# Block products of sums in two matmul stages, and a reordered stage before the recurrence, in a two-block fp32 kernel

## Chip, cores and metric

One core of a Trainium2 chip. The metric is the device time of one execution in microseconds (us), median of the runs. All data are fp32.

## The reference, cut to what matters

The program computes a first block (attention and a mixture of experts, two layers) and then a second block on the 512 tokens it leaves, with D = 1024. The change touches the end of the first block and two stages of the second:

```
h = rmsnorm(x, pre_mix_g)                              # x: result of the first block (layer norm of ALPHA * h_mid + gate * experts)
y_gla, y_sc, y_dil = recurrence(h), convolution(h), dilated_attention(h)
br = stack([y_gla, y_sc, y_dil])                       # each 512 wide
proj = einsum('bsgc,gcd->bsgd', br, w_branch)
gates = sigmoid(h @ w_gate + b_gate)                   # (512 x 1024) @ (1024 x 3072)
merged = sum(gates * proj, axis=2)
x = x + rmsnorm(merged @ w_mix_out, post_mix_g)
h = rmsnorm(x, pre_ffn_g)
gt = causal_dwconv(h @ w_ff_gate) + b
y = (gelu(gt) * (h @ w_ff_up)) @ w_ff_down             # (512 x 2816) @ (2816 x 1024)
x = x + rmsnorm(y, post_ffn_g)
```

## The kernel before

The program is a row of phases. Each phase is one block in which the queues SP, POOL, PE (TensorE), ACT (ScalarE) and DVE (VectorE) run their own hand-written lists of instructions, tied by semaphores; a phase begins when every queue has ended the one before. P = 128 partitions, C = 8 slices of the 1024 channels, NLAT = 4 tiles of 128 tokens, LAT = 512 tokens. `Steps` makes an engine wait for its own last instruction. Weights of the second block go through `ring`, two slots of 2 MB: job j lies in slot j % 2 (`load_weights`, L1983), and a load is issued by SP once the last product of job j - 2 is done.

**combine_turn_phase (L1772 to L1953)** ends the first block. For each token tile t it loads two rows of expert results and `h_mid` (L1804), weighs and adds them (ACT L1848, DVE L1892), multiplies by the gate, adds `h_mid` (L1895, L1896), takes the mean and variance (L1897 to L1899), normalises (ACT L1852, L1854; DVE L1903, L1904, L1911, L1912), takes the root of the mean square (ACT L1858, L1860), and turns the tile with PE by a product with a diagonal matrix `diag` that holds the inverse root (DVE L1919, L1920; PE L1950), after which ACT moves the eight turned pieces to `hT` (L1867). Between the turns PE computes the values of tiles 0 and 1 for the recurrence with ring slot 1 (`values`, L1942). SP issues the rows of tiles 0 and 1, the load of job 1, the first two rows of tile 2, ... in the order of L1802 to L1813, so job 1 stands ahead of tile 2 and job 0 ahead of tile 3 on its queue; then come 16 small loads for the recurrence (L1815 to L1828), on whose arrival it waits before it stores `h` (L1831).

**recurrent_phase and rope_phase** follow and are unchanged. The rope phase already computes its products in the form that the change brings to the gates, with seven block products in place of eight; for that it has made four sums of token halves, in the memory of `merged`.

**merge_phase (L2555 to L2769)** has 48 steps n in three branches i of 16. In the first 8 steps of a branch PE makes a gate chunk of 128 outputs (L2618: 8 matmuls of 128x512), which ACT takes with a sigmoid (L2689); in the next 8 a branch product (L2628: 4 matmuls), which DVE multiplies with the gates and adds to `merged` (L2737, L2740). Products go in turn to two PSUM banks `pa`. Into the even and odd steps up to n = 33 the dilated attention is woven, one unit u = n // 2 of head and query tile at a time: scores (PE L2636), mask and maximum (DVE L2749, L2752), exp (ACT L2694), scaling (DVE L2759), transposes (PE L2648), moves (ACT L2704), weighing of the values (PE L2661), taking (ACT L2709). POOL has nothing to do in this phase.

**feed_forward_phase (L2776 to L3097)**: mixing product (L2884), norms and transposes (L2894), then for each of NF = 22 chunks f of 128 hidden outputs the products of gate and up in seven block products (L2908: 28 matmuls of 256 columns), the first of them copied by ACT (L2990), all joined by DVE (`post`, L3055 to L3058), convolution (ACT L2992, DVE L3081, L3083), gelu (L2994), product (L3090). PSUM is four pieces `banks` of 1024 columns; chunk f uses pieces 0 and 1 where f is even, 2 and 3 where it is odd. The sums of weights are made by POOL for the first pair (L2835) and by DVE after that (L3067). The down product (L2941 to L2956) runs over PASSES = tiles (0, 1), then 2, then 3, each over the 22 chunks, with 1 MB of down weights per two chunks in four slots made of the ring (L2848); a tile's norm, residual and store follow (L2964 to L2965, L3094 to L3097, L2870).

Of the kernel before, what the change touches and what calls it, by code (L numbers as in the profile page):

```python
# [18 lines left out]
ALU = mybir.AluOpType  # L19
# [4 lines left out]
P = 128  # L24
# [1747 lines left out]
def combine_turn_phase(nc, g, l, share, gain, hT, rc):  # L1772
# [4 lines left out]
    with Phase(nc) as ph:  # L1777
# [6 lines left out]
        diag = ph.sb("diag", [P, 2, P])  # L1784
# [3 lines left out]
        row_in = ph.sems("row_in", NLAT)  # L1788
# [3 lines left out]
        weighted, var_ready, root_ready, norm_ready, n_ready, h_made, h_stored, rooted, scaled, turned, moved = (  # L1792
            ph.sem(n) for n in ("weighted", "var_ready", "root_ready", "norm_ready", "n_ready", "h_made", "h_stored", "rooted", "scaled", "turned", "moved"))
# [6 lines left out]
        def _(sp):  # L1800
            ph.clear_other_pool(sp)
            for t in range(NLAT):  # L1802
                for j, src in enumerate((g["y"][tile(t), :], g["y"][tile(t + NLAT), :], g["h_mid"][tile(t), :])):
                    sp.dma_start(y[:, t, j], src).then_inc(row_in[t], 16)  # L1804
                if t == 0:
                    sp.dma_start(gate[:], g["mods"][l, 0:1, 5 * D:6 * D].broadcast_to([P, D])).then_inc(gate_in, 16)
                if t == 2:
                    load_weights(sp, g, 0)
                if t == 1:
# [3 lines left out]
                    load_weights(sp, g, 1)  # L1813
# [26 lines left out]
        def _(act):  # L1840
# [4 lines left out]
            def weigh(t):  # L1845
                if t < NLAT:
                    act.wait_ge(row_in[t], 48)
                    act.activation(y[:, t, 0], y[:, t, 0], ACT.Copy, scale=share[:, t, 0:1]).then_inc(weighted, 1)  # L1848

            def norm(t):  # L1850
                act.wait_ge(var_ready, t + 1)
                act.activation(mv[:, t % 2, 2:3], mv[:, t % 2, 1:2], ACT.Sqrt, bias=eps[:, 0:1]).then_inc(root_ready, 1)  # L1852
# [3 lines left out]
            def root(t):  # L1856
# [3 lines left out]
                act.activation(ss[:, t % 2, 1:2], ss[:, t % 2, 0:1], ACT.Sqrt, scale=1.0 / D, bias=eps[:, 1:2]).then_inc(rooted, 1)  # L1860

# [19 lines left out]
            move(NLAT - 1)  # L1881

        @block.vector
        def _(dve):
# [9 lines left out]
            def residual(t):  # L1894
                step(dve.tensor_tensor(y[:, t, 0], y[:, t, 0], gate[:], ALU.mult))  # L1895
                step(dve.scalar_tensor_tensor(out=y[:, t, 0], in0=y[:, t, 2], scalar=ALPHA, in1=y[:, t, 0], op0=ALU.mult, op1=ALU.add))  # L1896
# [17 lines left out]
            def scale(t):  # L1914

                dve.wait_ge(rooted, t + 1)
                if t >= 2:
                    dve.wait_ge(turned, t - 1)
                step(dve.reciprocal(ss[:, t % 2, 1:2], ss[:, t % 2, 1:2]))  # L1919
                dve.tensor_scalar(diag[:, t % 2], g["ident"][:], ss[:, t % 2, 1:2], None, ALU.mult).then_inc(scaled, 1)  # L1920
# [12 lines left out]
            scale(NLAT - 1)  # L1933

        @block.tensor
        def _(pe):
            def values(t):
# [3 lines left out]
                for i in range(C):  # L1941
                    last = pe.matmul(pV[t][:], hT[:, i, tile(t)], ring[:, 1, i, :], start=(i == 0), stop=(i == C - 1))  # L1942
                last.then_inc(valued, 1)

            for t in range(NLAT):
# [609 lines left out]
def merge_phase(nc, g, hT, yT, QK, dv, merged, mask, bias):  # L2555
# [3 lines left out]
    NU = H * NLAT  # L2559

# [20 lines left out]
    with Phase(nc) as ph:  # L2581
# [11 lines left out]
        turned, moved, weighed, o_out, order = (ph.sem(n) for n in ("turned", "moved", "weighed", "o_out", "order"))  # L2593
        block = ph.block()
        ring, ring_in, ident = g["ring"], g["ring_in"], g["ident"]

        def last_output(j):
# [628 lines left out]
```

## Time and profile before

| | |
|---|---|
| median of 3 runs | 3357.71 us (3355.45 to 3358.58) |
| the profiled execution | 3354.14 us |
| its span in the trace | 3352.3 us |
| mean granted clock of TensorE | 0.945 of full speed |
| busy: PE, DVE, ACT, POOL | 85%, 37%, 23%, 16% of the span |

In the page, PE is a TensorE matmul and PEld the load of its stationary operand, which overlaps the matmul. An fp32 matmul leaves two records in the trace, a transpose one. Matmuls are pipelined, so the duration of one record (592 ns for 512 columns) is longer than the time from one to the next; the time of a stretch of matmuls divided by their count is the price of a record. Times of day are us from the start of the span.

### The profile page before, as it was taken

The page shows a single profiled execution, that of the slowest core. Times are in us where ns is not written, and L with a number is a line of the kernel's source. Part 1 is how long each engine was busy: PE and PEld are TensorE (multiplying, and loading weights), DVE is VectorE, ACT ScalarE, POOL GpSimd, SP SyncE. Part 2 cuts the span into 40 slices and gives each one's busy share as a digit, 9 for nine tenths or more (in the row PEclk, how much of TensorE's full clock was granted, in tenths as well). Part 3 has the DMA queues.
Part 4 walks back from the last instruction along what each step waited for, and adds up shares of the span by engine and source line. Part 5 has one row for each costly group of instructions (what it writes and reads, how often), then busy time and mean ns, then how long its engine had stood idle before and what let it go on. Part 6 is the DMA issues. An engine that isn't in the chain of part 4 may idle for free. (4 is left out here: it accounts for less than half of the span.)

```text
span 3352.3 us, 53098 instructions
## 1 busy us (share of the span) xinstructions
PE 2833.0 (85%) x21873; PEld 1738.4 (52%) x21873; DVE 1239.9 (37%) x2476; ACT 770.7 (23%) x1501; POOL 538.7 (16%) x664
## 2 busy tenths in 40 slices
PE   7998889588776698885867663899999999999999
PEld 4555655344343345653433332445886554588844
DVE  3424856311111343755111112634761331355501
ACT  2224651112111322630111111420212331211100
POOL 0003630233322001521323221010000000100000
PEclk9999999699998899997989887999999999999999
DMA  8833012999999652025999997221222112322337
GB/s 310 310 143 118 1 76 88 380 397 426 426 426 422 237 126 97 3 94 216 382 425 424 424 423 315 72 77 59 101 76 75 51 51 75 114 76 82 119 126 263
DMA packets 188535, 679.24 MB, mean 203 GB/s; under 512 B 52766, under 2 KB 94222, under 8 KB 163782
## 3 DMA queue, kind: packets, MB, share of 16 engines
q1 hardware_dynamic: 176446, 655.56, 50.2%
q0 software_dynamic: 11808, 21.03, 1.7%
q8 instruction: 134, 2.20, 0.3%
q14 instruction: 43, 0.35, 0.0%
q10 hardware_dynamic: 104, 0.10, 0.0%
HBM read 653.89 MB, written 33.98 MB: 205 GB/s over the span
## 5 line engine op out<-in xcount | busy, mean ns | idle before, releaser
L1756 DVE TENSOR_TENSOR hh<-hs,pH 128x128 f32<-128x128 f32 x118 | 33.9, 287 | 774.6 <-ACT hs L1739 774.6
L1719 PE MATMUL pH<-w,room 128*32 128x256 f32 x4224 | 253.9, 395 | 54.5 <-DMA w<-in_moe_w 54.2
L1719 PE MATMUL pH<-room 128*32 128x256 f32 x3328 | 213.5, 414 | 90.1 <-DMA room<-in_moe_w 67.0
L942 POOL TENSOR_SCALAR E<-E,st 128x768 f32<-128x768 f32 (+3 forms) x80 | 168.0, 2100 | 644.7 <-DVE st L1192 644.1
L1719 PEld LDWEIGHTS pH<-w,room 128*32 128x32 f32 x4224 | 140.8, 114 | 158.3 <-issue 77.2
L1719 PEld LDWEIGHTS pH<-room 128*32 128x32 f32 x3328 | 115.0, 120 | 181.0 <-issue 97.2
L419 PE MATMUL pa<-aT,w 128*128 128x512 f32 x416 | 205.8, 599 | 1.3 <-DVE aT L693 1.3
L1727 PE MATMUL pY<-w,hT 128*32 128x256 f32 x2112 | 129.2, 385 | 76.8 <-DVE hT L1759 61.0
L2618 PE MATMUL pa<-hT,ring 128*128 128x512 f32 x384 | 169.7, 598 | 0.0
L987 PE MATMUL pT<-ident,E 128*128 128x128 f32 x672 | 112.7, 287 | 54.9 <-ACT PT L1097 31.3
L2952 PE MATMUL banks<-ring,aT 128*128 128x512 f32 x352 | 151.2, 592 | 0.0
L1727 PE MATMUL pY<-room,hT 128*32 128x256 f32 x1664 | 100.6, 382 | 54.3 <-DVE hT L1759 54.3
L2094 PE MATMUL pa<-hT,ring 128*128 128x512 f32 x320 | 143.8, 606 | 0.0
L1017 PE MATMUL pS<-wout,oT 128*128 128x512 f32 x320 | 141.4, 594 | 0.8 <-issue 0.8
L1727 PEld LDWEIGHTS pY<-w,hT 128*32 128x32 f32 x2112 | 62.7, 110 | 142.8 <-DVE hT L1759 101.6
L1739 ACT ACTIVATE hs<-pH 128x128 f32<-128x128 f32 x118 | 32.7, 277 | 450.6 <-PE pH L1719 450.6
L1675 POOL DMA_INDIRECT y<-y,at_y x122 | 125.8, 1031 | 60.2 <-POOL at_y L1695 59.1
L1742 ACT ACTIVATE y<-pY 128x256 f32<-128x256 f32 x118 | 45.2, 383 | 346.2 <-PE pY L1727 340.7
L987 PEld LDWEIGHTS pT<-ident,E 128*128 128x128 f32 x672 | 71.3, 142 | 99.9 <-issue 47.5
L956 PE MATMUL pS<-room 64*128 64x256 f32 (+2 forms) x608 | 109.3, 476 | 8.3 <-ACT E L1086 4.9
L2618 PEld LDWEIGHTS pa<-hT,ring 128*128 128x128 f32 x384 | 72.4, 192 | 84.4 <-issue 84.4
L2952 PEld LDWEIGHTS banks<-ring,aT 128*128 128x128 f32 x352 | 66.9, 190 | 83.8 <-issue 83.7
(557 smaller groups left out, 4760.4 us busy)
## 6 DMA issues: line engine op xcount, KB each, us to landing
w<-in_moe_w SPq DMA_DIRECT2D x144, 2048.0 KB
room<-in_moe_w SPq DMA_DIRECT2D x48, 2048.0 KB
mw<-in_mod_w SPq DMA_DIRECT2D x24, 2048.0 KB, 16.6
ring<-in_w_ff_down SPq DMA_DIRECT2D x33, 1024.0 KB, 4.9
ring<-in_w_in SPq DMA_DIRECT2D x15, 2048.0 KB, 8.4
ring<-in_w_gate SPq DMA_DIRECT2D x6, 2048.0 KB, 8.4
wf<-in_w_ff_gate SPq DMA_DIRECT2D x11, 1024.0 KB, 5.7
wf<-in_w_ff_up SPq DMA_DIRECT2D x11, 1024.0 KB, 8.0
```

The source lines that it names most:

```text
L419: last = pe.matmul(pa[n % 2][:, 0:512], w[:, i % SLOTS_W, k, tile(c)], aT[:, k, 0:512], start=(k == 0), stop=(k == C - 1))
L942: pool.tensor_scalar(e, e, st[:, u % 4, 6 + b:7 + b], None, ALU.mult).then_inc(readyP, 1)
L956: return pe.matmul(pS[u % 2][:, at:at + w], qT[rows, p, tile(n)], kT[rows, k_chunk(p), k0:k0 + w], start=True, stop=True)
L987: last = pe.transpose(pT[:, tile(j)], E[:, u % NB, b, tile(i)], ident[:])
L1017: last = pe.matmul(pS[n % 2][:, half * 512:(half + 1) * 512], oT[:, k, tile(n)], wout[:, k, half * 512:(half + 1) * 512], start=(k == 4), ...
L1675: pool.indirect_dma_start(out=y_rows, out_offset=bass.IndirectOffsetOnAxis(ap=at_y[:, b:b + 1], axis=0), in_=y[:, b], in_offset=None, boun ...
L1719: last = pe.matmul(pH[strip(s), 0:2 * P].rearrange("p (j n) -> p j n", j=2), xT[:, k, :], slot_of(g, "w13", b)[:, :, k, s * P:(s + 1) * P] ...
L1727: last = pe.matmul(pY[strip(s), 0:YW], hT[:, k, :], slot_of(g, "w2", b)[:, k, s * YW:(s + 1) * YW], start=(k == 0), stop=(k == HC - 1))
L1742: act.activation(y[:, b], pY[:, 0:YW], ACT.Copy).then_inc(y_moved, 1)
L2094: last = pe.matmul(pa[b][:], ring[:, j % RING, i, tile(c)], hT[:, i, :], start=(i == 0), stop=(i == C - 1))
L2618: last = pe.matmul(pa[b][:], ring[:, j % RING, k, (c % 4) * P:(c % 4 + 1) * P], hT[:, k, :], start=(k == 0), stop=(k == C - 1))
L2952: last = pe.matmul(banks[b][:, h * 512:(h + 1) * 512], aT[:, f, tile(t)], wd[:, m % SLOTS_D, f % 2, h * 512:(h + 1) * 512], start=(f == 0) ...
```

## The change

Three parts, in one diff.

**Gates.** Two neighbouring gate chunks c, c + 1 of a branch, the two halves of the channels and the two halves of the tokens form a product of two by two blocks. It is computed with seven products of blocks (each 4 matmuls of 128x256) of sums, in place of eight blocks (16 matmuls of 128x512). DVE makes four sums of weights per pair ahead of it (`sums`, four operations of 512 elements; the last overwrites the weights in the ring); the four sums of tokens are those of the rope phase for branch 0 and are made by POOL (four operations of 1024 elements, in memory of Q and K that heads 0 and 1 no longer need) for branches 1 and 2. The seven products go to the two banks `pa` in four turns (two, two, two and one product). ACT copies the first of them (`copy_first`), DVE adds (`add_first`, three operations of 256 elements; `add_then`, two of 256 and one of 512), and ACT takes both sigmoids of a pair one after the other at the next even step.

**Down product.** Tiles 0 and 2 are computed together in one pass of 11 pairs of chunks, seven matmuls of 512 columns per pair in place of eight; tiles 1 and 3 follow in passes of their own, as tiles 2 and 3 did. DVE makes four sums of down weights per pair (`down_sums`, 512 elements each) and four sums of tokens in two goes (`down_tokens`, of 768 and 640 elements). The order of the rows out is 0, 2, 1, 3.

**The stage before the recurrence.** The rows of all four tiles stand ahead of both weight loads on SP's queue; `h_mid` has a semaphore of its own, so the weighing doesn't wait for it; the table of Sqrt is asked for at the start; the turn is a transpose of rows that ACT has scaled (`scale`) in place of a product with a diagonal; `gather` and the roots are moved earlier in the lists; the values of tile 1 are split round the turn of tile 3, and both copies of values come last.

```diff
@@ combine_turn_phase
             for t in range(NLAT):
                 for j, src in enumerate((g["y"][tile(t), :], g["y"][tile(t + NLAT), :], g["h_mid"][tile(t), :])):
-                    sp.dma_start(y[:, t, j], src).then_inc(row_in[t], 16)
+                    sp.dma_start(y[:, t, j], src).then_inc(mid_in[t] if j == 2 else row_in[t], 16)
...
-                if t == 2:
-                    load_weights(sp, g, 0)
...
-                    load_weights(sp, g, 1)
+            load_weights(sp, g, 1)
+            load_weights(sp, g, 0)
...
+            def scale(t):
+                act.wait_ge(inverse, t + 1)
+                act.activation(y[:, t, 1], y[:, t, 0], ACT.Copy, scale=ss[:, t % 2, 1:2]).then_inc(scaled, 1)
...
+            act.activation(warm[:], eps[:, 0:1], ACT.Sqrt)
             weigh(0)
             weigh(1)
+            deviation(0)
             for t in range(NLAT):
                 norm(t)
+                weigh(t + 2)
                 if t:
                     move(t - 1)
-                weigh(t + 2)
                 root(t)
-                if t >= 2:
-                    take_values(t - 2)
+                deviation(t + 1)
+                scale(t)
             move(NLAT - 1)
+            take_values(0)
+            take_values(1)
...
             residual(0)
+            gather(1)
             for t in range(NLAT):
-                gather(t + 1)
                 factors(t)
-                if t:
-                    scale(t - 1)
                 if t + 1 < NLAT:
                     residual(t + 1)
                 complete(t)
-            scale(NLAT - 1)
+                gather(t + 2)
+                invert(t)
...
                 for k in range(C):
-                    last = pe.matmul(pT[t % 2][:, tile(k)], y[:, t, 0, k::C], diag[:, t % 2], start=True, stop=True)
+                    last = pe.transpose(pT[t % 2][:, tile(k)], y[:, t, 1, k::C], g["ident"][:])
                 last.then_inc(turned, 1)
-                if 1 <= t <= 2:
-                    values(t - 1)
+                if t == 1:
+                    values(0, range(C))
+                if t == 2:
+                    values(1, range(C // 2))
+            values(1, range(C // 2, C))
@@ merge_phase, tensor
+                (a0, a1), (b0, b1) = weights(n)
+                t = token_sums(i)
+                pairs = (((a0, hT[:, lo, first]), (S[1], t[1])), ((S[0], t[0]), (S[2], hT[:, hi, then]))) if n % 2 == 0 else (
+                    ((a1, hT[:, hi, first]), (b0, t[2])), ((b1, t[3]),))
+                for pair in pairs:
+                    if q >= 2:
+                        pe.wait_ge(taken[q % 2], q // 2)
+                    for at, (w, x_cols) in enumerate(pair):
+                        if n % 2 == 0 and at:
+                            pe.wait_ge(s_made, GATES.index(n) // 2 + 1)
+                            if i:
+                                pe.wait_ge(t_made, 1)
+                        for k in range(C // 2):
+                            last = pe.matmul(bank(q)[:, at * HT:(at + 1) * HT], w[:, k, :], x_cols[:, k, :], start=(k == 0), stop=(k == C // 2 - 1))
+                    last.then_inc(product[q % 2], 1)
+                    q += 1
@@ merge_phase, vector
+                    if n < 48 and n % 16 < 8:
+                        add_first(n)
+                else:
+                    if n < 47 and (n + 1) % 16 < 8:
+                        sums(n + 1)
+                    if u < NU:
+                        scale(u)
+                    if n % 16 < 8:
+                        add_then(n)
@@ feed_forward_phase, tensor
+            for m in range(NP):
+                pe.wait_ge(wd_in[m % SLOTS_D], 16 * (m // SLOTS_D + 1))
+                pe.wait_ge(down_t, 1 if m < early_sums else 2)
+                pe.wait_ge(down_s, m + 1)
+                w, s = wd[:, m % SLOTS_D], wf_flat[:, m % 2]
...
+                    if m == 0 and name == "P5":
+                        pe.wait_ge(posted[1], NP)
+                    last = pe.matmul(down_at(name), x_rows, of_w, start=(m == 0), stop=(m == NP - 1))
+                last.then_inc(wd_used, 1)
@@ feed_forward_phase, vector
             for f in range(NF):
                 b, i = f % 2, f // 2 + 1
+                if f == NF - 1:
+                    dve.wait_ge(raised[1], NP - 1)
+                    down_tokens(0, 0, early_sums)
+                    down_sums(0)
                 post(f)
+                if f == NF - 1:
+                    down_sums(1)
...
+            for m in range(2, NP):
+                down_sums(m)
+                if m == early_sums - 2:
+                    down_tokens(1, early_sums, NP)
+            dve.wait_ge(first_taken, 1)
```

## Rows read from the trace of the kernel before

**Rows 1.** The chain of waits that ended last: start, us, what.

```profile
2887.66 0.88 PE banks L2894 x8
...
2949.26 244.78 PE banks L2908 x1120
3194.04 151.08 PE banks L2952 x352
```

**Rows 2.** Busy time by stretch: us, then PE, PEld, DVE, ACT, POOL busy, clock, DMA.

```profile
2066.30:2134.80 68.50, 30.29 (x96) 21.74 (x97) 32.96 (x50) 26.95 (x59) 0.55 (x3) 0.69 0.58 214
...
2546.90:2858.20 311.30, 309.29 (x996) 162.54 (x996) 80.05 (x152) 76.23 (x122) 0.00 (x0) 0.99 0.17 58
2858.20:2921.90 63.70, 62.98 (x168) 30.53 (x168) 17.14 (x32) 14.34 (x34) 10.66 (x4) 0.97 0.51 147
2921.90:3193.90 272.00, 267.21 (x1289) 236.29 (x1290) 151.74 (x200) 42.12 (x71) 0.00 (x0) 0.99 0.26 86
```

**Rows 3.** Groups by line and shape in the merge phase.

```profile
L2618 PE MATMUL pa<-hT,ring 128*128 128x512 f32 x384 | 169.7, 598 | 0.0
...
L2689 ACT ACTIVATE z<-pa,gate_bias 128x512 f32<-128x512 f32 x24 | 16.5, 688 | 53.6 <-PE pa L2618 53.6
L2694 ACT ACT_TABLE_LOAD x9 | 11.5, 1283 | 0.4 <-PEq L91 0.3
```

**Rows 4.** Timeline of a unit with ten keys in the merge phase.

```profile
2646.59 2.31 PE L2636 MATMUL pS<-QK 128*128 128x256 f32 x6
2649.37 1.08 ACT L2704 ACTIVATE PT<-pT 128x512 f32<-128x512 f32 x2 [5.74 <-PE pT L2648]
2649.61 3.60 PE L2628 MATMUL pa<-yT,ring 128*128 128x512 f32 x8
2651.37 1.36 ACT L2694 ACTIVATE E<-E,st 128x1280 f32<-128x1280 f32 x1 [0.91 <-DVE st L2753]
2653.04 1.95 PE L2661 MATMUL pO<-PT,dv 128*128 128x128 f32 x16
```

**Rows 5.** Timeline of the last chunks of the feed-forward phase and the first down products.

```profile
3160.80 1.22 DVE L3067 TENSOR_TENSOR S<-S,wf 128x1024 f32<-128x1024 f32 x1
...
3188.17 0.69 DVE L3090 TENSOR_TENSOR aT<-xg,r 128x512 f32<-128x512 f32 x1 [0.70 <-ACT xg L2994]
...
3193.87 21.62 PE L2952 MATMUL banks<-ring,aT 128*128 128x512 f32 x50
3194.07 0.38 ACT L2990 ACTIVATE r<-banks 128x256 f32<-128x256 f32 x1 [5.93 <-PE banks L2908]
3194.56 0.69 DVE L3055 TENSOR_TENSOR r<-r,banks 128x512 f32<-128x512 f32 x1 [5.70 <-ACT r L2990]
3195.28 0.42 DVE L3056 TENSOR_TENSOR r<-r,banks 128x256 f32<-128x256 f32 x1
...
3196.46 0.69 DVE L3058 TENSOR_TENSOR r<-r,banks 128x512 f32<-128x512 f32 x1
```

**Rows 6.** Timeline of the stage before the recurrence (SPq: issue of a transfer).

```profile
2073.42 1.15 ACT L1848 ACTIVATE y<-y,share 128x1024 f32<-128x1024 f32 x1 [14.61 <-DMA y<-h_mid]
2079.26 1.15 ACT L1848 ACTIVATE y<-y,share 128x1024 f32<-128x1024 f32 x1 [4.69 <-DMA y<-h_mid]
2090.66 1.15 ACT L1848 ACTIVATE y<-y,share 128x1024 f32<-128x1024 f32 x1 [6.91 <-DMA y<-h_mid]
2100.87 1.15 ACT L1848 ACTIVATE y<-y,share 128x1024 f32<-128x1024 f32 x1 [0.28 <-DMA y<-h_mid]
2105.94 14.89 SPq L1831 DMA_DIRECT2D h<-y  x4
2119.25 1.23 DVE L1912 TENSOR_TENSOR y<-y,lrow 128x1024 f32<-128x1024 f32 x1
2128.47 3.85 PE L1950 MATMUL pT<-diag,y 128*128 128x128 f32 x16
2132.35 2.17 ACT L1867 ACTIVATE hT<-pT,gcol 128x128 f32<-128x128 f32 x8 [3.09 <-PE pT L1950]
```

More of the change, by code:

```diff
@@ L2611, in gate @@
             def gate(n):
-                b, i, c = n % 2, n // 16, n % 16
-                j = GATE_JOB + 3 * i + c // 4
-                if n >= 2:
-                    pe.wait_ge(taken[b], n // 2)
-                pe.wait_ge(ring_in[j % RING], loads_of(j))
-                for k in range(C):
-                    last = pe.matmul(pa[b][:], ring[:, j % RING, k, (c % 4) * P:(c % 4 + 1) * P], hT[:, k, :], start=(k == 0), stop=(k == C - 1))
-                last.then_inc(product[b], 1)
+                i, q = n // 16, use(n)
@@ L2621, in branch @@
             def branch(n):
-                b, i, c = n % 2, n // 16, n % 8
+                q, i, c = use(n), n // 16, n % 8
                 j = GATE_JOB + 3 * i + 2
                 w = ring[:, j % RING].rearrange("p k n -> p (k n)").rearrange("p (k n) -> p k n", n=D)
-                pe.wait_ge(taken[b], n // 2)
+                pe.wait_ge(taken[q % 2], q // 2)
                 pe.wait_ge(ring_in[j % RING], loads_of(j))
                 for k in range(4):
-                    last = pe.matmul(pa[b][:], w[:, k, c * P:(c + 1) * P], yT[:, 4 * i + k, :], start=(k == 0), stop=(k == 3))
@@ L2629, in branch @@
-                last.then_inc(product[b], 1)
+                    last = pe.matmul(bank(q)[:], w[:, k, c * P:(c + 1) * P], yT[:, 4 * i + k, :], start=(k == 0), stop=(k == 3))
+                last.then_inc(product[q % 2], 1)
             def score(u):
@@ L2685, in _, with copy_first, take_gates @@
         def _(act):
-            def take_gate(n):
+            def copy_first(n):
+                q = use(n)
+                act.wait_ge(product[q % 2], q // 2 + 1)
+                if n:
+                    act.wait_ge(posted, GATES.index(n) // 2)
+                act.activation(p1[:], bank(q)[:, 0:HT], ACT.Copy).then_inc(copied, 1)
+            def take_gates(n):
                 i, c = n // 16, n % 16
-                act.wait_ge(product[n % 2], n // 2 + 1)
-                act.activation(z[:, c], pa[n % 2][:], ACT.Sigmoid, bias=bias[:, 8 * i + c:8 * i + c + 1]).then_inc(taken[n % 2], 1)
+                act.wait_ge(posted, GATES.index(n) // 2 + 1)
+                for c in (c - 1, c):
+                    act.activation(z[:, c], z[:, c], ACT.Sigmoid, bias=bias[:, 8 * i + c:8 * i + c + 1]).then_inc(z_ready, 1)
             def exp(u):
@@ L2734, in take_branch @@
                 i, c = n // 16, n % 8
[L2735 to L2737 removed]
+                to, q = merged[:, c] if i == 0 else t1[:], use(n)
+                dve.wait_ge(product[q % 2], q // 2 + 1)
+                dve.wait_ge(z_ready, 8 * i + c + 1)
+                dve.tensor_tensor(to, bank(q)[:], z[:, c], ALU.mult).then_inc(taken[q % 2], 1)
                 if i:
[L2739 removed]
+                    dve.wait_ge(taken[q % 2], q // 2 + 1)
                     step(dve.tensor_tensor(merged[:, c], merged[:, c], t1[:], ALU.add))
@@ L2943, in _ @@
+            for i, (t, b) in enumerate(((1, 3), (3, 0))):
                 for f in range(NF):
+                    m = (i + 1) * NP + f // 2
                     if f % 2 == 0:
                         pe.wait_ge(wd_in[m % SLOTS_D], 16 * (m // SLOTS_D + 1))
-                    pe.wait_ge(done[f % 2], f // 2 + 1)
-                    if m >= NP:
-                        pe.wait_ge(done[0], NP)
-                        pe.wait_ge(done[1], NP)
-                    for t, b in zip(tiles, to):
-                        for h in range(2):
-                            last = pe.matmul(banks[b][:, h * 512:(h + 1) * 512], aT[:, f, tile(t)], wd[:, m % SLOTS_D, f % 2, h * 512:(h + 1) * 512],
-                                             start=(f == 0), stop=(f == NF - 1))
+                    for h in (1, 0):
+                        if f == 0 and h == 0 and i == 0:
+                            pe.wait_ge(first_taken, 1)
+                        if f == 0 and i == 1:
+                            pe.wait_ge(down_posted, 1)
+                        last = pe.matmul(banks[b][:, h * 512:(h + 1) * 512], aT[:, f, tile(t)], wd[:, m % SLOTS_D, f % 2, h * 512:(h + 1) * 512],
+                                         start=(f == 0), stop=(f == NF - 1))
```

197 lines of the change are left out of this document (150 added, 47 removed).

## The prediction

> **What bounds the kernel now.** I read the chain of waits first. It ends in the feed-forward phase, and its long pieces are matmuls without a gap: 1120 records of L2908 in 244.78 us, 352 of the down product in 151.08 us [rows 1]. That gives the two prices on which the sum rests: 151.08 / 352 = 0.4292 us for a record of 512 columns and 244.78 / 1120 = 0.2186 us for one of 256; a matmul has two records. The second row is a block product of the very form that the change brings elsewhere, with its weight loads, so the price of the short form needs no guess. The busy time by stretch says what holds each stage [rows 2]: PE is busy for 309.29 of the 311.30 us of the merge phase at a clock of 0.99 (nothing else matters there: DVE works 80 us, ACT 76, POOL nothing), and for 30.29 of 68.50 us ahead of the recurrence, at a clock of 0.69. There no engine is the bound. The timeline shows ACT waiting for rows four times, the last two arrivals at 2090.7 and 2100.9 us behind 2 MB of weights each, and then a long tail from the end of the last h to the end of the last move [rows 6].
>
> **Gates.** Before: 384 records of 512 columns [rows 3], 384 x 0.4292 = 164.8 us. After: 12 pairs x 7 products x 4 matmuls x 2 = 672 records of 256 columns, 672 x 0.2186 = 146.9 us. PE saves 17.9 us, all on its path, if nothing new holds it.
>
> What is added lies on other engines. DVE per pair: four sums of weights, three adds of 256 and two of 256 and one of 512 elements. At 0.69 us for 512 and 0.42 for 256 [rows 5] that is 2.8 + 1.3 + 1.5 = 5.6 us, 12 times, 67 us on top of 80 of 311: it fits. ACT gains a copy of 256 (0.38 us [rows 5]) per pair; its sigmoids are as many as before (0.69 us each, with table loads of 1.28 [rows 3]).
>
> The new waits are the ones to price, since a bank is now used four times per pair of steps in place of twice, and the first use comes back only through ACT and DVE. I take the largest unit. It begins its scores at 2646.59, the branch product starts 3.0 us later, the moves end at 3.9 and exp starts at 4.8 [rows 4]. In the changed order PE has its third turn (bank 0 again) after 3.0 us, two turns of 16 records (3.5 each) and the weighing of 1.95 [rows 4] with the last transposes: at about 12.3 us. ACT reaches its copy after the moves (3.9), a table and two sigmoids (6.5), a table, exp of 1.36 with its 0.19 of accumulator (9.4) and the copy (9.8); DVE hands the bank back at 10.3. There are 2 us to spare. Bank 1 needs two adds after the second turn (11.2) and is wanted at 15.8. The sums for the next pair and the scaling of exp end at 15.1, as the third turn's products come, so the next pair's are ready long before their use. The tightest place is branch 2, steps 32 to 39, where no attention lies between: a pair lasts 12.2 us, bank 0 must be back 1.75 us after its second use, and the two adds take 1.15 us and two hand-overs of 0.1 to 0.2. I cost the new waits at nothing there; if the slack is gone, the price is some 0.3 us at 4 pairs, and in the pairs with units 1 us at 8 pairs at most. At the very start PE needs the first four sums, 2.8 us after DVE starts, and has its first score and first product, some 2.5 us: 0.4 us lost. Gain taken: **17.5 us**, bounds 9 and 18.
>
> POOL's four token sums start when the scores of unit 7 are done (step 14) and are wanted by the second product of step 16. PE has between them two branch products (3.4 each), weighings, transposes, a small score and the first gate product, about 13 us. POOL took 10.66 us for four such operations of 1024 elements [rows 2]. They fit with some 2 us over. The Trainium skill, page "SBUF — State Buffer", section on who interferes with whom, speaks against this: a DVE operation with two SBUF inputs and a GpSimd operation that reads SBUF lock each other out for a whole instruction. DVE's four sums for step 16 (2.8 us) fall into that span; by that rule POOL ends about 1 us late once, and the sum would be 1 us less; no row here shows the two together.
>
> **Down product.** Before: 352 records of 512. After: 11 x 7 x 2 = 154 and, for tiles 1 and 3, 2 x 22 x 2 x 2 = 176, together 330: 141.6 us. PE saves 9.4 us. Loads stay 33 of 1 MB, the fastest use (3.4 us per MB) is as before in the two single passes and slower (6.0 us) in the first, so they stay hidden. DVE's four sums per pair (2.8 us) hide behind 6.0 us of matmuls. The start does not hide. The product of chunk 20 is done at 3188.86, then DVE takes `down_tokens`: four operations of 768 elements, between 0.69 and 1.22, say 0.96 each [rows 5], to 3192.8, and `down_sums(0)`, 2.8, to 3195.7. PE is ready at 3193.87 and waits **1.8 us** for it. Behind it on DVE stands `post(21)`, 2.6 us, to 3198.3, needed at the fifth product of the first pair, 3195.7 + 3.4 = 3199.1: covered by 0.8 us. `down_sums(1)` ends at 3201.2, wanted at 3201.7; the convolution, gelu and product of chunk 21 end near 3204, `down_sums(2)` at 3207, wanted at 3207.7; after that there are 3 us to spare per pair. Between the passes PE has one free matmul of 0.86 us to cover a copy of 0.6 with its hand-over. The tail after the last matmul is the same list of work. Gain: 9.4 - 1.8 = **7.6 us**, bounds 5 (each of the three thin covers fails by a microsecond) and 9.4.
>
> **The stage before the recurrence.** DVE is busy 32.96 us for four tiles, 8.2 each [rows 2], and now waits for data in between. With the weights behind, tile 2's rows come 2.6 MB after tile 1's (two broadcasts and the rows), at the 0.34 to 0.40 MB/us of the arrivals seen near 2086.5, tile 3's near 2091, ring job 1 near 2096, job 0 near 2101. DVE then never waits for rows after tile 1. Tile 0 starts 1.3 us earlier, as it doesn't wait for `h_mid`. Walking the two lists with the durations seen, DVE waits about 1.4 us for each root at tiles 0, 1, 2 or for the norm behind it, 6 us in all, and the last h is ready at 2111.3; now it is at 2120.5 [rows 6]. The tail: now ACT moves tile 2 first, then comes the root, and PE is at values(1) until 2128.5, turns for 3.85, moves for 2.17: 14.0 us. After: move of tile 2 to 2112, root 1.5, scaling 1.15 (a row of 1024 as in L1848), turn of 8 records in place of 16, between 0.88 us (L2894, warm [rows 1]) and 2.1 (half of 3.85 at the low clock), I take 2.1 because PE stands idle ahead of it; then four matmuls of values, 3.4, and a copy of 0.6: 2121.2. The stage ends at 2134.5 now. Gain **13.3 us**.
>
> SP's queue is passed too: the 16 small loads now stand behind both weight loads, so the wait for them ends near 2110 (2105.9 now), and only then do four stores of h go out, 2 MB in some 6 us, to about 2118. That is 3 us before the phase ends, so it costs nothing; with job 0 or the small loads 5 us later it would set the end. Bounds 8 (that, or a lower clock in the values) and 15.
>
> **Sum.** 17.5 + 7.6 + 13.3 = 38.4 us off the profiled execution's 3354.14 = 3315.7; the median of the runs stands 3.6 above that execution, so 3319.3 as a median. What differs by 0.2% (7 us) either way can't be told from no change.
>
> **Rivals.**
> 1. *The bank hand-over becomes the bound of the gates* (slower). If ACT's and DVE's work between the uses of a bank does not lie beside the products, each pair pays the copy, six adds and four sums, 6.0 us, and in the 8 pairs with units tables, sigmoids and exp, 5.5 us: 12 x 6.0 + 8 x 5.5 = 116 us less the 38 gained, 3436 us. It decides from 38.4 / 12 = 3.2 us of idle PE per pair; my walk has none. For it: only two banks. Against: a margin of 2 us in the largest unit. Chance 0.04.
> 2. *The margin in the pairs is thin by a microsecond*: half the gate's gain goes, 17.5 to 9: 3328. Chance 0.07.
> 3. *The transfers end the stage ahead of the recurrence*: SP's stores or ring job 1 hold it, 13.3 to 8: 3325. For it: the queue now carries 4 MB ahead of the small loads. Chance 0.11.
> 4. *A stage moved earlier collides*: the recurrence, started 13 us sooner, waits for a load it didn't wait for and gives the gain back: 3333. Its DMA share is 0.2 or so and its first two jobs have landed, so 0.02.
>
> **Numbers.** The forecast has 0.76, 3314 to 3325 by its own bounds. Range 3313 to 3330 takes in rivals 2 and 3. Faster by over 0.2%: 0.95, within it 0.01, slower 0.04.
>
> **What would show it.** In the profile after: L-rows of the gates with 672 records of 256 columns and no idle PE on `taken`; the gate phase at 294 us in place of 311; the pause of PE before the first down product near 1.8 us, for DVE; 330 records of down products; the stage before the recurrence at 55 us, ACT waiting for DMA twice in place of four times. A PE idle time of over 1 us per pair in the merge phase, or an end of the early stage set by SP, would make it wrong.

## The result, and the profile after

| | before | after |
|---|---|---|
| median | 3356.58 us (4 runs, 3355.01 to 3358.58) | 3314.53 us (4 runs, 3310.92 to 3315.24) |
| profiled execution / its span | 3354.14 / 3352.3 us | 3315.24 / 3313.1 us |
| ratio | | 0.9872, 95% interval 0.9855 to 0.9889 |

The change takes 42 us off, 1.28% (1.11 to 1.45%); 38.4 were forecast, and 3314.5 lies in the range, near its lower end: the three upper bounds together (18 + 9.4 + 15) would have given 3315.3. The two traces are compared stage by stage. First the busy time by stretch of the kernel after, with the columns of [rows 2]: stage ahead of the recurrence, recurrence and rope, merge, feed-forward up to the first down product, down products.

```profile
2068.40:2121.60 53.20, 20.43 (x64) 11.21 (x64) 31.68 (x46) 31.37 (x64) 0.56 (x3) 0.67 0.76 276
2121.60:2533.60 412.00, 399.92 (x2340) 279.52 (x2340) 221.80 (x314) 79.46 (x113) 16.27 (x22) 0.99 0.22 76
2533.60:2827.60 294.00, 289.06 (x1284) 217.12 (x1284) 146.93 (x272) 80.83 (x134) 10.28 (x4) 0.99 0.17 62
2827.60:3163.90 336.30, 328.89 (x1456) 266.18 (x1456) 175.99 (x241) 56.84 (x106) 9.73 (x4) 0.99 0.31 97
3163.90:3305.20 141.30, 141.26 (x329) 62.54 (x330) 47.36 (x64) 7.50 (x13) 0.00 (x0) 1.00 0.65 227
```

| stage | before | after | change | forecast |
|---|---|---|---|---|
| all ahead of the changed stage | 2066.3 | 2068.4 | +2.1 | 0 |
| ahead of the recurrence | 68.5 | 53.2 | -15.3 | -13.3 |
| recurrence and rope | 412.1 | 412.0 | -0.1 | 0 |
| merge | 311.4 | 294.1 | -17.3 | -17.5 |
| feed-forward to the end | 494.0 | 485.4 | -8.6 | -7.6 |
| span | 3352.3 | 3313.1 | -39.2 | -38.4 |

In the merge phase PE's records went from 996 to 1284, DVE's busy time from 80 to 147 us, and the stage got 17.3 us shorter: the matmuls have half the columns. The two unchanged stretches differ by 0.1 us (recurrence and rope) and by 2.1 us (the first block). The latter is scatter: in the twelve other profiled executions below, whose first blocks are all the same code, the stage ahead of the recurrence begins anywhere between 2064.8 and 2071.0 us. So single executions can't be compared to better than some 6 us. Stages compare better, though not perfectly: the unchanged recurrence and rope lasts from 408.9 to 412.4 us in the fourteen traces.

For 512 columns the price is that of [rows 1]. This is the chain of waits of the kernel after, beside them.

```profile
2917.02 232.94 PE banks L3052 x1064
...
3163.94 66.33 PE banks L3096 x154
3230.27 75.64 PE banks L3108 x176
```

66.33 / 154 = 0.4307 us and 75.64 / 176 = 0.4298 us per record of 512 columns, against 0.4292 taken; together 142.0 us, 141.6 forecast.

The price of 256 columns was taken too high. Timeline (PE alone) of the kernel before, at the start of the 244.78 us on which the price rests, and then of two neighbouring pairs of gates in the kernel after, with no attention between them:

```profile
2949.26 6.50 PE L2908 MATMUL banks<-hT,wf 128*128 128x256 f32 x16 [3.45 <-DVE wf L3067]
2955.59 1.89 PE L2908 MATMUL banks<-merged,S 128*128 128x256 f32 x8
...
2773.82 1.89 PE L2679 MATMUL pa<-hT,ring 128*128 128x256 f32 x8
2785.91 1.89 PE L2679 MATMUL pa<-hT,ring 128*128 128x256 f32 x8
```

A pair of 56 records takes 12.09 us, 0.2159 per record and not 0.2186. In the kernel before a chunk of 56 records takes the same 12.09 us once it runs (2967.68 to 2979.77). But its first 16 records, behind a pause of 3.45 us, took 6.33 us in place of 3.45, at a granted clock of 0.55, and the division by 1120 spread that over all.

### The profile page after: what moved, and what is told of

The parts are those of the page before. It is cut to its first block and busy times, and to the rows that moved or that the text cites. A ratio compares the mean times of both kernels' runs of the same rounds, so it can differ in the third digit from the quotient of the medians.

```text
span 3313.1 us, 53803 instructions
## 1 busy us (share of the span) xinstructions
PE 2797.7 (84%) x22107; PEld 1780.7 (54%) x22107; DVE 1347.6 (41%) x2648; ACT 780.2 (24%) x1519; POOL 548.0 (17%) x668
## 5 line engine op out<-in xcount | busy, mean ns | idle before, releaser
L1727 PE MATMUL pY<-room,hT 128*32 128x256 f32 x1664 | 100.6, 382 | 54.3 <-DVE hT L1759 54.3
L2105 PE MATMUL pa<-hT,ring 128*128 128x512 f32 x320 | 143.8, 606 | 0.0
L1669 POOL COPY at_x<-gather_at 128x1 int32 (+1 forms) x124 | 22.8, 184 | 511.3 <-DVE room L1748 493.6
L1727 PEld LDWEIGHTS pY<-room,hT 128*32 128x32 f32 x1664 | 48.7, 109 | 106.1 <-DVE hT L1759 79.3
L419 PEld LDWEIGHTS pa<-aT,w 128*128 128x128 f32 x416 | 78.4, 191 | 43.3 <-issue 36.6
L2105 PEld LDWEIGHTS pa<-hT,ring 128*128 128x128 f32 x320 | 61.1, 194 | 75.1 <-issue 74.8
```

Of the source, the lines that this page charges most:

```text
L419: last = pe.matmul(pa[n % 2][:, 0:512], w[:, i % SLOTS_W, k, tile(c)], aT[:, k, 0:512], start=(k == 0), stop=(k == C - 1))
L1727: last = pe.matmul(pY[strip(s), 0:YW], hT[:, k, :], slot_of(g, "w2", b)[:, k, s * YW:(s + 1) * YW], start=(k == 0), stop=(k == HC - 1))
L2105: last = pe.matmul(pa[b][:], ring[:, j % RING, i, tile(c)], hT[:, i, :], start=(i == 0), stop=(i == C - 1))
```

## Where PE waits now

PE's waits in the merge phase of the kernel after: who waited for whom, us in total, times, longest.

```profile
PE pS L2698 <- PEq L91: 4.5, 1, 4.5
PE pT L2710 <- DVE E L2831: 2.9, 2, 2.7
```

The 4.5 us are the start of the phase, as before. There is no wait of L2679 (the gates) for a bank. What is there instead is a pause of 2.72 us in front of the transposes of unit 7. Its timeline:

```profile
2633.11 2.89 POOL L2655 TENSOR_TENSOR QK<-hT,QK 128x1024 f32<-128x1024 f32 x1
2633.11 0.68 DVE L2841 TENSOR_TENSOR cos<-ring 128x512 f32<-128x512 f32 x1
2633.82 2.72 DVE L2842 TENSOR_TENSOR sin<-cos,ring 128x512 f32<-128x512 f32 x1
...
2636.08 2.67 POOL L2656 TENSOR_TENSOR QK<-hT,QK 128x1024 f32<-128x1024 f32 x1
2636.58 2.72 DVE L2843 TENSOR_TENSOR s<-ring,sin 128x512 f32<-128x512 f32 x1
...
2640.13 0.89 DVE L2831 TENSOR_SCALAR E<-E,st 128x1280 f32<-128x1280 f32 x1
...
2641.08 1.09 PE L2710 MATMUL pT<-ident,E 128*128 128x128 f32 x8 [2.72 <-DVE E L2831]
```

Two of DVE's weight sums take 2.72 us in place of 0.69. Each ends 0.55 us after the end of the POOL operation that was under way (2636.54 against 2636.00, 2639.30 against 2638.75). The scaling of exp stands behind them on DVE's list, so it is 4.1 us late, and PE, which had 1.3 us to spare, stands for the rest.

The trace of the kernel before already holds such a meeting, the other way round, in the very four POOL operations from which the prediction took 10.66 us:

```profile
2878.41 1.22 DVE L3039 TENSOR_TENSOR x<-x,r 128x1024 f32<-128x1024 f32 x1
2878.56 3.29 POOL L2835 TENSOR_TENSOR S<-wf 128x1024 f32<-128x1024 f32 x1 [580.57 <-DMA wf<-in_w_ff_up]
```

DVE started first and took its usual 1.22 us; POOL started 0.15 us later and took 3.29 us, where its third operation there, with DVE still, takes 2.34.

The start of the down products, timeline:

```profile
3159.75 0.96 DVE L3230 TENSOR_TENSOR S<-aT,S 128x768 f32<-128x768 f32 x1
...
3163.10 0.69 DVE L3220 TENSOR_TENSOR ring<-ring 128x512 f32<-128x512 f32 x1
3163.71 0.68 DVE L3237 TENSOR_TENSOR r<-r,banks 128x512 f32<-128x512 f32 x1
3163.94 1.10 PE L3096 MATMUL banks<-ring,aT 128*128 128x512 f32 x2 [1.91 <-DVE ring L3220]
```

This is the forecast step: 0.96 us for 768 elements, a pause of 1.91 (1.8 forecast). No later down product waits.

The stage ahead of the recurrence, timeline, to be read beside [rows 6]:

```profile
2073.65 1.15 ACT L1847 ACTIVATE y<-y,share 128x1024 f32<-128x1024 f32 x1 [3.75 <-DMA y<-y]
2079.98 1.15 ACT L1847 ACTIVATE y<-y,share 128x1024 f32<-128x1024 f32 x1 [5.18 <-DMA y<-y]
2086.45 1.15 ACT L1847 ACTIVATE y<-y,share 128x1024 f32<-128x1024 f32 x1 [2.22 <-DMA y<-y]
2093.27 1.13 ACT L1847 ACTIVATE y<-y,share 128x1024 f32<-128x1024 f32 x1
2107.15 5.79 SPq L1830 DMA_DIRECT2D h<-y  x4
2111.37 1.23 DVE L1924 TENSOR_TENSOR y<-y,lrow 128x1024 f32<-128x1024 f32 x1
2116.11 1.16 PE L1958 MATMUL pT<-ident,y 128*128 128x128 f32 x8 [1.57 <-ACT y L1867]
2117.11 3.60 PE L1949 MATMUL pV<-ring,hT 128*128 128x512 f32 x8
2117.31 2.17 ACT L1874 ACTIVATE hT<-pT,gcol 128x128 f32<-128x128 f32 x8 [1.25 <-PE pT L1958]
2120.74 0.60 ACT L1842 ACTIVATE rc_gv<-pV 128x512 f32<-128x512 f32 x1 [0.78 <-PE pV L1949]
```

Counted from the stage's start, the last h is ready at 44.2 us (2112.60 - 2068.4) in place of 54.2, and the tail from there is 9.0 us in place of 14.3 (to the first matmul of the recurrence). ACT waits for rows three times, for tiles 0, 1 and 2, where the prediction had two; the third wait, 2.22 us, holds nobody, since DVE comes to tile 2's rows only at 2089.19.

## The experiments: the three parts alone

Three kernels, each the kernel before with one of the three functions of the diff put in whole (and, for the gates, the two further arguments of its call).

**Early stage alone.** 

> The kernel before with the reordered stage ahead of the recurrence alone. Theory (the parts are independent, each worth its own stage): that stage lasts 53.2 us as in the profile after, in place of 68.5, the other stages are unchanged, and the whole is 15 us (0.45%) faster. Rival (the early stage's gain is partly given back later, by loads or by the clock at the start of the recurrence): the stretch from its end to the merge phase is over 412 us and the whole gains under 12 us.

Measured: ratio 0.9950 (0.9936 to 0.9963), 17 us. In its trace the stage lasts 53.1 us and the stretch behind it 412.2:

```profile
2065.10:2118.20 53.10, 20.32 (x64) 11.23 (x64) 31.68 (x46) 31.36 (x64) 0.53 (x2) 0.67 0.76 276
```

Nothing is given back later. The stretch is 0.1 us longer than in the kernel before (412.1). The prediction's fourth rival is out.

**Gates alone.** 

> The kernel before with the seven block products of the gates alone. Theory: the merge phase lasts 294.1 us in place of 311.3, 17 us (0.51%) faster in all, and DVE's two sums beside POOL's token sums again take 2.7 us each with a pause of PE of 2.7 us once. Rival (the three parts help one another, e.g. through the clock): under 14 us.

Measured: ratio 0.9954 (0.9940 to 0.9967), 15 us. The merge phase lasts 294.9 us (16.5 less), and PE has the same 2.7 us of pause there. The part carries its own gain and its own loss.

**Down products alone.** 

> The kernel before with the seven block products of the down stage alone. Theory: the stretch from the first mixing product to the end is 494.1 - 9.3 + 1.9 = 486.7 us if the 1.7 us that the mixing product gained in the profile after came from the clock that the new merge phase leaves, and 485.4 if it came from anything else; the whole is 7 to 9 us (0.2 to 0.27%) faster. Rival (the first pass of the down product is worth less than counted): 4 us or less.

Measured: ratio 0.9987 (0.9978 to 0.9996) over 11 runs, which is 4.4 us with 1.3 to 7.4 from the interval: less than the 7 to 9 expected, with only the interval's end above 7, and too small for runs that scatter by 14 us to size. The trace sizes it: the chain of the down products is 142.0 us (66.33 + 75.64) in place of 151.1, and a pause of 1.9 us stands ahead of it, which leaves 7.2. From the mixing product to the end it is 484.1 in place of 494.0. Neither of my two figures for that stretch was met, since it varies by itself: the same unchanged code, from the mixing product to the first down product, takes 335.6 us in the kernel before, 334.6 with the early stage alone, 332.9 with the gates alone. Two places in the traces account for it, both with slow matmuls. The mixing product up to the first transposes takes 29.2 us in some executions and 27.5 in others. And behind PE's pause of 3.45 us at the second pair of chunks the first records cost 2.9 us extra in the kernel before, 3.1 in the kernel after (granted clock 0.50 there), 1.8 with the early stage alone and 0.1 with the gates alone (clock 1.00), at the same pause. Whether the change has a part in the 1.7 us that the kernel after gained at the mixing product is open: the three executions without the new merge phase have 29.2, of the eleven with it four have 29.2 and seven 27.5. So it does not force the faster start, and three executions are too few to say whether it favours it.

The three ratios together make 1.09%, against 1.28% (1.11 to 1.45%) for all: parts that simply add, within what the measurement can tell.

## The experiments: DVE beside POOL

**POOL's token sums left out.**

```diff
             pool.wait_ge(scored, 3 * 2 * NLAT)
-            step(pool.tensor_tensor(T1[2], ...))
-            step(pool.tensor_tensor(T1[0], ...))
-            step(pool.tensor_tensor(T1[1], ...))
-            pool.tensor_tensor(T1[3], ...).then_inc(t_made, 1)
+            pool.sem_inc(t_made, 1)
```

> The kernel after, with POOL's four sums of token halves left out, so branches 1 and 2 of the gates multiply whatever lies there; all else runs as before. Theory A (DVE's sums of two SBUF operands stand still while POOL works on SBUF operands): the two sums of 2.72 us at step 15 take 0.69 us, PE's pause of 2.72 us ahead of the transposes of unit 7 is gone, and the merge phase lasts 294.1 - 2.7 = 291.4 us. Rival B (they are slow because a load is landing in the ring slot that they read, or for the order of the steps): they stay at 2.7 us and the phase at 294.

Measured: the merge phase lasts 291.1 us. Groups of DVE around step 15, as busy, mean ns:

```profile
L2839 DVE TENSOR_TENSOR sin<-cos,ring 128x512 f32<-128x512 f32 x1 | 0.7, 691 | 0.0
L2840 DVE TENSOR_TENSOR s<-ring,sin 128x512 f32<-128x512 f32 x1 | 0.7, 691 | 0.0
```

and PE's wait there:

```profile
PE pT L2707 <- DVE E L2828: 0.2, 1, 0.2
```

Same operations, same data in the ring, same place in the list, and no slow one. Theory A stands: it is POOL's work that holds them.

**DVE's first sums of a branch two steps earlier.**

```diff
-                    if n < 47 and (n + 1) % 16 < 8:
+                    if n % 16 < 7:
                         sums(n + 1)
+                    elif n in (13, 29):
+                        sums(n + 3)
```

> The kernel after, with DVE's four weight sums for the first pair of branches 1 and 2 made at step 13 of the branch before in place of 15, when POOL does not work yet. Theory A: they take 0.69 us each, the scaling of unit 7, which now falls beside POOL, is late by under 3 us and that is covered, PE's pause is gone, merge phase 291.5 us. Rival B: the pause stays, 294 us. Rival C (the scaling is held instead, for as long): a pause of 1 us or more stays.

Measured: merge phase 290.7 us, no wait of PE but the phase's start. The scaling of unit 7 now falls beside POOL:

```profile
2634.26 2.35 POOL L2655 TENSOR_TENSOR QK<-hT,QK 128x1024 f32<-128x1024 f32 x1
2634.43 2.86 DVE L2831 TENSOR_SCALAR E<-E,st 128x1280 f32<-128x1280 f32 x1
```

It takes 2.86 us in place of 0.89 and costs nothing, because PE wants it only 2 us later. Both expectations of theory A are met. So the scaling, which reads one large operand in SBUF (and a column of factors) and writes to SBUF, is held as well as the sums, which read two. Beside POOL's first two operations DVE ran operations of 0.69 us with a PSUM operand and a reduction (1.49 us) at full speed.

## The experiments: how much the bank hand-over can take

ACT gets k more copies of 208 elements, to memory that nobody reads, ahead of `copy_first`.

```diff
+                for _ in range(k):
+                    pause(act.activation(idle_act[:], mask[2][:, 0:208], ACT.Copy))
                 act.activation(p1[:], bank(q)[:, 0:HT], ACT.Copy).then_inc(copied, 1)
```

**k = 2.** 

> The kernel after, with two more ACT copies (to memory nobody reads) ahead of the copy of the first product in each pair, 0.8 us more before bank 0 is handed back. Prediction's reading (2 us to spare in the largest unit, nothing on the path): merge phase unchanged at 294 us. Rival (the hand-over is already on the path): 12 x 0.8 = 9 us longer.

Measured: 294.0 us, no new wait of PE. There is room for 0.8 us.

**k = 8.** 

> The kernel after, with eight more ACT copies ahead of the copy of the first product in each pair, 3.1 us more. Prediction's reading (slack of 1.2 to 2 us per pair): PE now pauses 1 to 2.3 us at some 10 pairs, the merge phase is 14 to 18 us longer, about 310, which is as long as the phase before. If the slack were 3 us or more, no change; if there were none, 37 us longer.

Measured: 313.8 us, 19.7 longer, slightly over the expected 14 to 18. PE's waits:

```profile
PE pa L2680 <- DVE t L2860: 14.1, 10, 2.1
```

Ten pauses, 14.1 us together, of 0.8 to 2.1 us: with 3.2 us put in, the slack was between 1.1 and 2.4 us in these ten pairs and there was no pause in the other two. The prediction's walk had 2 us for the largest unit. The experiment delays only the hand-over that goes through ACT's copy; the slack of the others, among them the one that the prediction called the tightest, was not measured, only that PE never waits for them. The loss is more than the pauses. In the timeline of the first long one

```profile
2559.16 3.21 ACT L2757 ACTIVATE idle_act<-dil_mask 128x208 f32<-128x208 f32 x8
...
2563.39 3.35 PE L2680 MATMUL pa<-hT,ring 128*128 128x256 f32 x8 [2.08 <-DVE t L2860]
```

the eight records behind a pause of 2.08 us take 3.35 us in place of 1.89, at a granted clock of 0.57. The pause of 2.72 us at unit 7, which the kernel after has too, is here followed by slow records as well:

```profile
2652.67 1.97 PE L2711 MATMUL pT<-ident,E 128*128 128x128 f32 x8 [2.72 <-DVE E L2836]
```

1.97 us in place of 1.09, at a clock of 0.61; in the kernel after the clock behind the same pause is 1.00. Behind another pause here, of 2.07 us, the clock is 1.00 too. So the same pause is sometimes paid once and sometimes with 1.6 us on top. What decides between these is left open.

## The experiments: the stage ahead of the recurrence

**Weight loads back at their old places on SP's queue.**

```diff
             for t in range(NLAT):
...
+                if t == 2:
+                    load_weights(sp, g, 0)
                 if t == 1:
...
+                    load_weights(sp, g, 1)
-            load_weights(sp, g, 1)
-            load_weights(sp, g, 0)
```

> The kernel after, with the two weight loads of the stage ahead of the recurrence back at their old places on SP's queue (job 1 ahead of tile 2's rows, job 0 ahead of tile 3's). Theory A (most of the gain is that rows no longer wait behind weights): rows of tiles 2 and 3 come 22 and 32 us after the stage's first rows again, and the stage lasts 62 to 65 us in place of 53.2. Rival B (the gain is in the lists of ACT, DVE and PE, and the rows' arrival was covered): 55 us or less.

Measured: 59.5 us, between the two theories. The timeline:

```profile
2090.28 1.15 ACT L1848 ACTIVATE y<-y,share 128x1024 f32<-128x1024 f32 x1 [7.05 <-DMA y<-y]
...
2099.14 1.15 ACT L1848 ACTIVATE y<-y,share 128x1024 f32<-128x1024 f32 x1 [3.76 <-DMA y<-y]
...
2115.90 1.23 DVE L1925 TENSOR_TENSOR y<-y,lrow 128x1024 f32<-128x1024 f32 x1
```

The rows come late as before (23.2 and 32.1 us after the stage's start at 2067.1), but the last h is ready at 50.0 us and not at 54.2. The queue order is worth 6.2 us on top of the other changes, and those take 9.1 us off the 68.5 with the rows as late as before.

**The turn as a product with a diagonal.**

```diff
-                    last = pe.transpose(pT[t % 2][:, tile(k)], y[:, t, 1, k::C], g["ident"][:])
+                    last = pe.matmul(pT[t % 2][:, tile(k)], y[:, t, 0, k::C], diag[:, t % 2], start=True, stop=True)
```

with DVE making `diag` behind the inverse root, and ACT's `scale` left out.

> The kernel after, with the turn in the stage ahead of the recurrence again a product with a diagonal matrix made by DVE, in place of ACT's scaling and a transpose. Theory A (the turn's form matters little; the 9.1 us that the stage gains at the old queue order come from the order of the lists): the stage lasts 53 to 55 us in place of 53.2, since 1.15 us of ACT is saved per tile and 1 to 2 us of PE added. Rival B (the transpose is what shortens the tail): 57 us or more.

Measured: 59.9 us (the recurrence's first matmul at 2130.20, the stage's start at 2070.3). My theory A is wrong and rival B right. The last h is ready at 44.2 us, as in the kernel after; all is lost in the tail:

```profile
2112.86 3.84 PE L1960 MATMUL pT<-diag,y 128*128 128x128 f32 x16
...
2120.85 4.18 PE L1960 MATMUL pT<-diag,y 128*128 128x128 f32 x16 [0.71 <-DVE diag L1930]
2124.82 4.45 PE L1951 MATMUL pV<-ring,hT 128*128 128x512 f32 x8
```

A turn takes 3.84 or 4.18 us there and 1.04 or 1.16 in the kernel after. Two stand one behind the other on the last tile's path: the turn of tile 2, whose move ACT does ahead of tile 3's root, and that of tile 3. The last four matmuls of values take 4.45 us there and 3.60 in the kernel after, another 0.9.

The clock is not what makes the product slow. Three turns, the first of the kernel before, then tiles 0 and 2 of the kernel after:

```profile
2094.27 4.12 PE L1950 MATMUL pT<-diag,y 128*128 128x128 f32 x16 [35.96 <-DVE diag L1920]
...
2092.28 1.97 PE L1958 MATMUL pT<-ident,y 128*128 128x128 f32 x8 [32.18 <-ACT y L1867]
2110.06 1.04 PE L1958 MATMUL pT<-ident,y 128*128 128x128 f32 x8
```

The product took 4.12 us at a granted clock of 0.52, and its last turn [rows 6] 3.85 us at 1.00. The transpose took 1.97 us at 0.50 and 1.04 at 1.00. Nor is it the number and size of the records: sixteen of 128 columns take 1.95 us in the merge phase [rows 4]. What differs is the stationary operand, every eighth element of a row in the turn (`y[:, t, 0, k::C]`) and contiguous in the merge phase; that this is the reason was not tried.

**The values of tile 1 in one piece.**

```diff
                 if t == 2:
-                    values(1, range(C // 2))
-            values(1, range(C // 2, C))
+                    values(1, range(C))
```

> The kernel after, with the values of tile 1 computed in one piece ahead of the turn of tile 3, as before. Theory A: the turn of tile 3 waits for them, some 1.7 us later, the last copy is the move of tile 3 and two short ones, and the stage lasts 54.2 us in place of 53.2. Rival B (the split is what shortens the tail, together with the clock): 57 us or more.

Measured: 54.3 us (2124.64 - 2070.37), as theory A had it. The split is worth 1.0 us (54.27 against 53.23). 6.2 + 6.7 + 1.0 = 13.9 of the 15.3 us. Each was taken out of the kernel after by itself, so they need not add up. The rest (the table load, `h_mid` on a semaphore of its own, `gather` and the roots earlier, the copies of values last) was not tried apart.

## The experiments: the two pauses taken out

**Token sums of the down product one chunk earlier.**

```diff
-                if f == NF - 1:
+                if f == NF - 2:
                     dve.wait_ge(raised[1], NP - 1)
                     down_tokens(0, 0, early_sums)
+                if f == NF - 1:
                     down_sums(0)
```

> The kernel after, with DVE's token sums for the down product one chunk earlier, into its idle time ahead of chunk 20's joining, and the first weight sums alone ahead of chunk 21's. Theory: PE's pause of 1.91 us before the first down product is gone, the stretch from the first mixing product to the end lasts 483.5 us in place of 485.4. Rival (the later joining of chunk 20 or 21 holds the fifth product): a pause of 1 us or more comes back there.

Measured: 483.9 us with a mixing start of 29.2 us in this execution (27.5 in the kernel after), so 1.7 us are masked in that figure, and the slow stretch behind the 3.45 us pause was 1.4 us shorter in it; the trace has the first down product at 3158.73 with no wait ahead of it, and the joining of chunk 21 at 3159.34 in time. The pause is gone and did not move.

**Both moves.** 

> The kernel after with both of these moves (first weight sums of branches 1 and 2 at step 13; token sums of the down product one chunk earlier). Theory: 2.6 us less in the merge phase and 1.9 us less at the down product, together 4.5 us (0.13%) faster than the kernel after, 43 us (1.3%) faster than the kernel before. Rival (one pause only moves): 2 us or less.

Measured: 3308.58 us (4 runs, 3300.80 to 3312.11), ratio to the kernel before 0.9852 (0.9834 to 0.9869), 49 us by medians. Its stretches for merge and for feed-forward up to the down products:

```profile
2533.80:2824.20 290.40, 288.38 (x1284) 217.09 (x1284) 144.98 (x272) 80.70 (x134) 9.89 (x4) 0.99 0.18 63
2824.20:3158.10 333.90, 328.40 (x1456) 266.07 (x1457) 175.92 (x240) 56.48 (x105) 9.73 (x4) 0.99 0.31 98
```

290.4 against 294.0 and 333.9 against 336.3, with the same mixing start: 3.6 + 2.4 = 6.0 us less in these stages than in the kernel after. The pauses account for 2.7 + 1.9 of it. Neither moved: PE waits at neither place. This version beats both kernels by its stages; against the kernel after the intervals of the ratios overlap (0.9834 to 0.9869 and 0.9855 to 0.9889), so the runs alone don't settle it.

## Why the prediction was right, point by point

- **Prices.** 330 records at 0.4292 us held (0.4302 measured). 672 at 0.2186 did not: they cost 0.2159, as the form's twin in the feed-forward phase does, 145.1 us in place of 146.9. The price had a slow start of 2.9 us in it, of a chain that I had read as matmuls without a gap.
- **Bank hand-over costed at nothing.** Right: no wait for a bank in the trace, unchanged with 0.8 us more, pauses of 0.8 to 2.1 us with 3.2 more. The first and second rival did not come.
- **First four sums, 0.4 us at the start.** In the trace PE goes from its first product (2534.71, slow clock) to the second (2537.79) without a wait: nothing lost. I had priced the first product at the full clock.
- **POOL's token sums "fit with some 2 us over".** This step failed. I asked only whether POOL would be late, 1 us at most by the page's rule, and took DVE's 5.6 us per pair as free. POOL was hardly held (2.89 and 2.67 us where it had 2.34 to 2.36); DVE was, by 4.1 us, and behind it the scaling that PE waits for. The Trainium skill, "SBUF — State Buffer", section on who interferes with whom, says that the one which starts first gets the pair for the whole instruction and the other blocks; by that rule it was DVE's turn to block as soon as its operation started later, which the trace agrees with: 2.72 us in place of 0.69, twice. The price was 2.7 us in place of the 1 that I named. I had also written that no row shows the two engines together; the row of 10.66 us does (3.29 us for its first operation, see above), with POOL as the one that started later and paid. In the gates POOL started first, and DVE paid.
- **Start of the down products: 1.8 us**; measured 1.91. The thin covers behind it (0.8, 0.5, 0.7 us) all held.
- **The early stage: 13.3 us**, bounds 8 and 15; measured 15.3. The term "turn of 8 records ... I take 2.1 because PE stands idle ahead of it" was mis-sized: it measured 1.04 for tile 2 and 1.16 for tile 3, both at a granted clock of 1.00, and 1.97 for tiles 0 and 1 at 0.50, for which PE had idled 32.2 and 6.4 us. Ahead of the last two turns stand the values, with 0 and 1.57 us of idle. That is 1.0 of the 2.0 us; the last h came 0.8 us sooner than walked, and the old stage ended 0.3 us later than I had read. "Half of 3.85 at the low clock" was a misreading that came out right for tiles 0 and 1 by luck: the 3.85 us were taken at a clock of 1.00. That the turn's form would matter I did not see even after the result, and the diagonal experiment showed it: 6.7 us.
- **SP's queue.** Forecast: small loads done near 2110, stores to 2118, 3 us to spare. In the trace the stores are issued from 2107.15 to 2112.94 (2.1 us later on this clock by the stage's start), and the stage ends with ACT's last copy. The third rival did not come.
- **The sum.** 38.4 forecast, 39.2 in the span. By stages, against the forecast: +2.1 of scatter in the first block, -2.0 ahead of the recurrence, -0.1 in the recurrence, +0.2 in the merge, -1.0 from the feed-forward on, where the mixing start alone gives -1.7. The merge came within 0.2 us although the pauses, which put PE's records off by 3.2 us, were not in its forecast. The traces show what made up for them: 1.8 us from the price of 256 columns, 0.9 from the start of the phase (the scores and first records at a low clock cost 3.3 us beyond full speed before and 2.4 after; why they differ is not shown), and the 0.4 us for the first sums. 17.9 + 1.8 + 0.9 - 3.2 = 17.4, against 17.3 measured. That the merge hit its figure is luck: two errors of nearly the same size and opposite sign.

## What to carry to other kernels

Take the price of a new form of product from a twin in the same trace, from one repetition to the next and not over a chain that begins behind a pause, and spend the effort on what each joined bank or operand costs the engines behind it. When work moves to an idle POOL, list what DVE does in those microseconds and what stands behind it on DVE's list. On a tail, look at the operation that occurs once per tile and stands twice in a row on the last tile's path.

## What the runs showed of the hardware

- A DVE operation on SBUF operands that starts while POOL works on SBUF operands ends 0.55 to 0.7 us after POOL's (for 0.69 us of own work): 2.72, 2.72 us, and 2.86 for the scaling of 1280 elements with one large operand (0.89 alone); 0.69 with POOL still. Where DVE started first (1.22 us), POOL took 3.29 us in place of 2.35.
- Eight fp32 transposes of 128x128 take 1.04 us at a granted clock of 1.00 and 1.97 at 0.50; the same turn as eight matmuls (16 records) takes 3.85 us at 1.00 and 4.12 at 0.52.
- Behind a pause of 3.45 us at the same place of the same code the granted clock was 0.50 in one execution, 0.55 in another and 1.00 in a third, and the first records cost between 0.1 and 3.1 us extra. Behind a pause of 2.72 us it was 1.00 in the kernel after and 0.61 in the run with eight more copies.
